# Retention's input projection in three passes on split operands, and the residual norms in two parts

## The chip, the cores and the metric

The kernel runs on one NeuronCore of a Trainium2 chip. The metric is the device time in microseconds (us) of one execution, as the median of several runs. The engines are TensorE (PE, with its weight loads as PEld), VectorE (DVE), ScalarE (ACT), GpSimd (POOL) and SyncE (SP), which issues most of the loads. Each runs its own instruction stream, and they meet only at semaphores.

## The reference, cut to what matters

Two blocks run one after the other on 512 tokens of width 1024. The first has two layers. A layer computes a mixer and then a feed-forward network, and each of the four is followed by a residual and a layer norm:

```python
for i in range(DEPTH):
    mod = (e @ ada_w[i] + ada_b[i])[:, None, :]
    sh1, sc1, g1, sh2, sc2, g2 = jnp.split(mod, 6, axis=-1)
    y = mixers[i % N_MIXERS](x * (1.0 + sc1) + sh1)
    x = layer_norm(DN_ALPHA * x + (1.0 + g1) * y, ln_g[i, 0], ln_b[i, 0])
    y = conv_ffn(x * (1.0 + sc2) + sh2, ffn_up[i], ffn_conv_w[i], ffn_conv_b[i], ffn_down[i])
```

(the second layer norm of a layer follows `conv_ffn` in the same way). The mixer of layer 1 is `retention`. Its input projection is `q, k, v, gate = jnp.split(h @ w_in, ...)`, with 1024 + 1024 + 2048 + 2048 columns: q and k are then turned by a rotary table, v is used by token, and gate goes through silu. The second block (a Hyena and HGRN2 mixer and a mixture of experts with 64 experts) is not touched by the change.

## The kernel before

Activations lie transposed in SBUF: `k.xT` holds the residual stream and `k.hT` the modulated input of the next matrix product, each as 8 tiles (KD) of 128 features by 512 tokens (T). Weights come in chunks through a ring of 4 slots (`NSLOT`): SP issues the load of chunk n as soon as chunk n-4 is used (`chunk_used`).

Most products of the first block use **split operands**. ACT rounds a chunk of weights to the matmul's reduced type (`round_chunk`, L373), POOL subtracts to get what is left and writes it back into the slot (`lower_chunks`, L378), and `SplitInput` does the same to the activations, tile by tile: ACT rounds (L455), DVE subtracts (L460). `products` then sums three passes for each input tile r: upper weights by upper input (L467), upper by lower (L468), lower by upper (L469). The projections of retention do without: `RetentionIn` multiplies plain 32-bit operands (L1460 by feature, L1471 by token), which TensorE runs as several passes inside. It takes 24 chunks of 256 columns: 8 for q and k (two groups of 128 features by 512 tokens each), 8 for v (by token: four groups of 128 tokens by 256 columns, so the weights move), 8 for gate (as q and k).

The order of stages is res0, up0, down0, rin (`RetentionIn`), heads, res1, up1, down1 and then the second block (`prepend` first). res0, down0, res1 and down1 are all `ResidualNorm`: 8 output tiles j of a product with 8, 22, 16 or 22 input tiles, each added to xT by DVE (L1237), and then the layer norm. In the norm PE sums the 8 tiles of xT to a mean (L1221), DVE subtracts it (L1245), ACT squares (L1268), PE sums the squares (L1225), ACT takes Ln and Exp (L1270, L1272), DVE scales (L1249), ACT applies gain and bias (L1275) and writes the modulated hT (L1285), and DVE multiplies xT by a constant (L1254). All stages end in `k.meet`, at which the four compute engines wait for one another. up0 and up1 are `FeedForwardUp`: 22 chunks, with convolution and gating on DVE (L1376, L1379, L1386), and in up0 a further table product on DVE (L680). Both start by splitting hT into their input.

## Time and profile before

| | |
|---|---|
| median of 3 runs | 4009.57 us (4006.97 to 4014.61) |
| the profiled execution's own time | 4000.63 us |
| its span in the profile | 3998.8 us |
| mean granted TensorE clock | 0.906 |

The profile is of one execution. Its rows give a start and a duration in us for an instruction (or for several alike, with xN), and in brackets how long the engine sat idle before it and whose signal ended that. A matmul's printed duration overlaps with its neighbours': what one costs in a row of many is the distance between starts. A plain 32-bit matmul appears as two records. res0 ends near 740, up0 runs to 1007, down0 with its norm to 1177, rin from 1184 to 1517, res1 with its norm to 1778, up1 to 2033, down1 with its norm to 2197, and the experts from about 2950 to the end.

### The profile page before, as it was taken

The page shows a single profiled execution, that of the slowest core. Times are in us where ns is not written, and L with a number is a line of the kernel's source. Part 1 is how long each engine was busy: PE and PEld are TensorE (multiplying, and loading weights), DVE is VectorE, ACT ScalarE, POOL GpSimd, SP SyncE. Part 2 cuts the span into 40 slices and gives each one's busy share as a digit, 9 for nine tenths or more (in the row PEclk, how much of TensorE's full clock was granted, in tenths as well). Part 3 has the DMA queues.
Part 4 walks back from the last instruction along what each step waited for, and adds up shares of the span by engine and source line. Part 5 has one row for each costly group of instructions (what it writes and reads, how often), then busy time and mean ns, then how long its engine had stood idle before and what let it go on. Part 6 is the DMA issues. An engine that isn't in the chain of part 4 may idle for free. (4 is left out here: it accounts for less than half of the span.)

```text
span 3998.8 us, 39863 instructions
## 1 busy us (share of the span) xinstructions
PE 3358.3 (84%) x15238; PEld 2171.1 (54%) x15238; DVE 1141.5 (29%) x1835; ACT 837.6 (21%) x1147; POOL 761.7 (19%) x363
## 2 busy tenths in 40 slices
PE   6988887799879998779988876899868888888886
PEld 3766775588744844558876775744343333333332
DVE  3524543566212002332231223544131111111112
ACT  2333223422220112332232333210100000000001
POOL 1422232233410001224442310200001111111110
PEclk8998888899989999889999875789979999999998
DMA  5233000355212212112230310110239999999996
GB/s 210 85 117 125 0 0 21 123 192 190 72 47 81 77 53 52 32 53 95 94 101 19 97 53 0 62 45 0 115 147 408 412 420 410 408 405 411 402 404 266
DMA packets 246141, 630.37 MB, mean 158 GB/s; under 512 B 18693, under 2 KB 192038, under 8 KB 221041
## 3 DMA queue, kind: packets, MB, share of 16 engines
q1 hardware_dynamic: 235249, 618.81, 41.1%
q0 software_dynamic: 10240, 8.43, 0.7%
q10 hardware_dynamic: 576, 2.10, 0.1%
q8 instruction: 49, 0.80, 0.1%
q14 instruction: 27, 0.22, 0.0%
HBM read 633.47 MB, written 20.97 MB: 164 GB/s over the span
## 5 line engine op out<-in xcount | busy, mean ns | idle before, releaser
L467 PE MATMUL ps<-arena_parts,arena_parts 128*128 128x512 f32 (+1 forms) x2016 | 750.6, 372 | 146.9 <-DVE hT_parts L460 65.5
L469 PE MATMUL ps<-arena_parts,ring_parts 128*128 128x512 f32 (+1 forms) x2016 | 743.7, 369 | 0.0
L378 POOL TENSOR_TENSOR ring_parts<-ring,arena_parts 128x2048 fp32r<-128x2048 f32 (+1 forms) x104 | 521.6, 5015 | 1085.7 <-ACT arena_parts L373 1085.7
L2773 PE MATMUL ps<-arena 128*64 128x512 f32 x1024 | 516.8, 664 | 161.4 <-DMA arena<-in_w_up 103.6
L468 PE MATMUL ps<-hT_parts,arena_parts 128*128 128x512 f32 (+1 forms) x1472 | 526.7, 358 | 0.0
L2774 PE MATMUL ps<-arena 128*64 128x512 f32 x1024 | 518.3, 665 | 0.0
L467 PEld LDWEIGHTS ps<-arena_parts,arena_parts 128*128 128x128 f32 x2016 | 383.5, 190 | 225.3 <-issue 112.9
L469 PEld LDWEIGHTS ps<-arena_parts,ring_parts 128*128 128x128 f32 x2016 | 383.4, 190 | 68.8
L2773 PEld LDWEIGHTS ps<-arena 128*64 128x64 f32 x1024 | 150.0, 152 | 496.0 <-issue 494.0
L468 PEld LDWEIGHTS ps<-hT_parts,arena_parts 128*128 128x128 f32 x1472 | 279.6, 190 | 41.1
L373 ACT ACTIVATE arena_parts<-ring 128x2048 fp32r<-128x2048 f32 (+1 forms) x104 | 208.8, 2008 | 382.4 <-PE ps L469 324.8
L2853 DVE TENSOR_SCALAR arena<-ps 128x256 f32<-128x256 f32 x64 | 27.2, 424 | 854.4 <-PE ps L2784 854.4
L1460 PE MATMUL ps<-hT,ring 128*128 128x512 f32 x512 | 222.4, 597 | 22.3 <-DMA ring<-in_ret_w_in 22.3
L2793 PE MATMUL ps<-arena 128*64 128x512 f32 x1024 | 233.8, 598 | 1.1 <-DVE arena L2853 0.6
L2693 POOL DMA_INDIRECT y_rows<-ring,y_of x64 | 64.7, 1011 | 855.4 <-ACT ring L2831 840.1
L468 PE MATMUL ps<-arena_parts,arena_parts 128*128 128x512 f32 x544 | 217.1, 399 | 0.0
L1460 PEld LDWEIGHTS ps<-hT,ring 128*128 128x128 f32 x512 | 98.0, 192 | 146.1 <-issue 146.0
L2837 ACT ACTIVATE arena<-ps 64x512 f32<-64x512 f32 x64 | 38.1, 595 | 649.0 <-PE ps L2774 649.0
L2774 PEld LDWEIGHTS ps<-arena 128*64 128x64 f32 x1024 | 149.9, 152 | 0.0
L2793 PEld LDWEIGHTS ps<-arena 128*64 128x64 f32 x1024 | 68.2, 136 | 114.8 <-issue 110.6
L2688 POOL DMA_INDIRECT ring<-x_rows,x_of x64 | 61.3, 958 | 334.5 <-DVEq L287 302.8
L1237 DVE SCALAR_TENSOR_TENSOR xT<-ps,mod,xT 128x512 f32 (+1 forms) x32 | 24.0, 751 | 332.1 <-PE ps L469 332.1
(446 smaller groups left out, 4028.0 us busy)
## 6 DMA issues: line engine op xcount, KB each, us to landing
arena<-in_w_gate SPq DMA_DIRECT2D x64, 2048.0 KB, 18.1
arena<-in_w_up SPq DMA_DIRECT2D x64, 2048.0 KB, 22.5
arena<-in_w_down SPq DMA_DIRECT2D x64, 2048.0 KB, 23.1
ring<-in_ffn_up SPq DMA_DIRECT2D x44, 1024.0 KB, 5.1
arena<-in_ada_w SPq DMA_DIRECT2D x20, 2048.0 KB, 9.9
ring<-in_ret_w_in SPq DMA_DIRECT2D x24, 1024.0 KB, 5.1
ring<-in_ffn_down SPq DMA_DIRECT2D x16, 1408.0 KB, 7.0
ring<-in_gdn_w_in SPq DMA_DIRECT2D x16, 1024.0 KB, 5.8
```

The costliest lines, as they stand in the source:

```text
L373: act.activation(self.upper(room, n, kt, cols), self.slot(n, kt, cols), ACT.Copy).then_inc(self.core.sem("chunk_rounded"), 1)
L378: pool.tensor_tensor(self.lower(n, kt, cols), self.slot(n, kt, cols), self.upper(room, n, kt, cols), ALU.subtract)\
L467: pe.matmul(out, upper[:, r], self.upper[r][:, part], start=(r == 0), stop=False)
L468: pe.matmul(out, upper[:, r], self.lower[r][:, part], start=False, stop=False)
L469: ins = pe.matmul(out, lower[:, r], self.upper[r][:, part], start=False, stop=(r == self.tiles - 1))
L1460: ins = pe.matmul(k.ps[:, g % 4, :], w[:, r, f * P:(f + 1) * P], k.hT[:, r, 0:T], start=(r == 0), stop=(r == KD - 1))
L2688: return pool.indirect_dma_start(m.xe[u], None, k.x_rows, at, bounds_check=T - 1, oob_is_err=False)
L2693: return pool.indirect_dma_start(k.y_rows, at, m.y_halves[u], None, bounds_check=2 * CHOICES - 1, oob_is_err=False)
L2773: pe.matmul(k.ps[upper, 2 + u, :], m.xeT[u][:, r, :], m.w_up[u][:, r, :], start=(r == 0), stop=(r == KD - 1))
L2774: ins = pe.matmul(k.ps[lower, 2 + u, :], m.xeT[u][:, r, :], m.w_gate[u][:, r, :], start=(r == 0), stop=(r == KD - 1))
L2793: ins = pe.matmul(k.ps[(upper, lower)[h], 6, :], m.actT[u][:, r, :], m.w_down[u][:, r, half], start=(r == 0), stop=(r == D_EXP // P - 1))
L2837: act.activation(m.silu[u], k.ps[SLOTS:2 * SLOTS, 2 + u, :], ACT.Silu).then_inc(self.sem("silu"), 1)
```

## The change

`RetentionIn` now uses split operands as well. ACT rounds and POOL subtracts each of its 24 chunks, and q, k and gate go through `products`. v is computed in four **pairs** of chunks: both chunks move together as 512 columns against 128 tokens of the input, again in three passes, into one bank for each group of 128 tokens. The first four chunks are loaded before the rope table and without waiting for the stage.

`ResidualNorm` is taken apart. While the product of the last output tile runs, PE sums the first seven tiles of xT with one matmul over a running total that DVE keeps (`origin`), and DVE and ACT centre and square those seven (centred on the mean of 7 tiles). The meet comes then, and a second part without a meet (`vector_tail`, `scalar_tail`, `tensor_tail`) adds and centres the last tile, corrects by the rest of the mean, takes the variance, and scales. ACT applies one combined gain and shift for each tile, twice (`upper` of the next stage's input, already rounded, and hT), and DVE subtracts to get `lower`. So up0, rin and up1 find their input split, and `prepend` no longer copies xT to hT. The first chunk of each following stage is rounded and split in the last chunk of the stage before (`following`; in `FeedForwardUp` the first chunk of the down projection).

```diff
+            if between and r == self.tiles // 2:
+                between()
             if first:
...
+        def origin():
+            self.wait(pe, "totalled", 1)
+            pe.matmul(k.ps[:, self.ORIGIN, :], k.ones[:], self.total, start=True, stop=True).then_inc(self.sem("mean"), 1)
...
-        self.wait(pe, "added", self.BANKS + KD)
-        for j in range(KD):
-            ins = pe.matmul(k.ps[:, 6, :], k.mean[:], k.xT[:, j, :], start=(j == 0), stop=(j == KD - 1))
-        ins.then_inc(self.sem("mean"), 1)
-        for j in range(KD):
-            self.wait(pe, "squared", j + 1)
-            pe.matmul(k.ps[:, 7, :], k.mean[:], self.square[:, j % 2], start=(j == 0), stop=(j == KD - 1)).then_inc(self.sem("var"), 1)
...
+        k = self.k
+        self.wait(pe, "centred", KD)
+        pe.matmul(k.ps[:, self.REST, :], k.mean[:], k.xT[:, KD - 1, :], start=True, stop=True).then_inc(self.sem("mean"), 1)
+        self.wait(pe, "totalled", 2)
+        pe.matmul(k.ps[:, self.VAR, :], k.mean[:], self.total, start=True, stop=True).then_inc(self.sem("var"), 1)
...
+    def centre(self, dve, j):
+        k = self.k
+        dve.scalar_tensor_tensor(k.xT[:, j, :], k.ps[:, self.ORIGIN, :], -1.0 / (D - P), k.xT[:, j, :], ALU.mult, ALU.add)\
...
+                self.add(dve, stream, n, c, f)
+                if j == 0:
+                    continue
+                a = k.xT[:, 0, :] if j == 1 else self.total
+                if j > 1:
+                    st.wait()
+                ins = dve.tensor_tensor(self.total, a, k.xT[:, j, :], ALU.add)
+                if j < KD - 2:
+                    st.done(ins)
+                else:
+                    ins.then_inc(self.sem("totalled"), 1)
...
+        stream.each(dve, self.chunks, self.per, tile, True)
         self.wait(dve, "mean", 1)
+        for step in range(KD + 1):
+            if step < KD - 1:
+                self.centre(dve, step)
+            if step >= 2:
+                self.add_square(dve, step - 1) if step < KD else None
...
+           .then_inc(self.sem("added"), 1)
         self.wait(dve, "added", self.BANKS + KD)
+        self.centre(dve, j)
+        self.add_square(dve, j)
+        self.wait(dve, "squared", KD + 1)
+        self.wait(dve, "summed", KD - 1)
+        dve.scalar_tensor_tensor(self.total, self.square[:, 0], -float(KD), self.total, ALU.mult, ALU.add).then_inc(self.sem("totalled"), 1)
         for j in range(KD):
-            dve.tensor_tensor(k.xT[:, j, :], k.xT[:, j, :], k.ps[:, 6, :], ALU.subtract).then_inc(self.sem("centred"), 1)
+            ins = dve.tensor_tensor(k.xT[:, j, :], k.xT[:, j, :], k.ps[:, self.REST, :], ALU.subtract)
+        st.done(ins)
+        st.wait()
         self.wait(dve, "rooted", 2)
+        for step in range(KD + 2):
...
+        if self.first:
+            self.input.scalar(act)
+        for c in range(self.first, self.chunks):
             stream.round_chunk(act, self.upper, stream.n + c, 0, self.kt, self.per * P)
             if c == 0:
                 self.input.scalar(act)
+        if self.following:
+            stream.round_chunk(act, self.upper, stream.n + self.chunks, 0, *self.following)
...
+    def scalar_tail(self, act):
+        k = self.k
+        self.take_square(act, KD - 1)
+        self.wait(act, "mean", 2)
+        self.wait(act, "summed", KD - 2)
+        act.activation(self.square[:, 0], k.ps[:, self.REST, :], ACT.Square).then_inc(self.sem("squared"), 1)
+        act.activation(self.one, k.eps[:, 0:1], ACT.Ln)
+        self.wait(act, "var", 1)
+        act.activation(self.inv, k.ps[:, self.VAR, :], ACT.Ln, bias=k.eps[:, 0:1]).then_inc(self.sem("rooted"), 1)
...
+            if self.next_input:
+                act.activation(self.next_input.upper[j], k.xT[:, j, :], ACT.Identity, bias=b, scale=a)
+            act.activation(k.hT[:, j, shown], k.xT[:, j, :], ACT.Identity, bias=b, scale=a).then_inc(self.sem("shifted"), 1)
...
-        self.input.vector(dve)
...
+                stream.round_chunk(act, self.upper, n + 1, i, FT, P)
...
+        def rope():
+            k.stage_over(sp, 9)
+            k.load_tables(sp, "rope", [(self.rope, k.tables["t_rope"])])
+
+        self.stream.load_run(sp, [tiles_of(k.ins["ret_w_in"])], KD, 2 * P, 3 * self.RUN, after_round=rope)
...
-                    for r in range(KD):
-                        ins = pe.matmul(k.ps[:, g % 4, :], w[:, r, f * P:(f + 1) * P], k.hT[:, r, 0:T],
-                                        start=(r == 0), stop=(r == KD - 1))
+                    at = slice(f * P, (f + 1) * P)
+                    ins = self.input.products(pe, k.ps[:, g % 4, :], upper[:, :, at], lower[:, :, at], first + g == 0)
...
+            stream.split_landed(pe, n + 1, 0, 2 * p + 1)
...
-                    ins = pe.matmul(k.ps[:, 4 + t, 0:2 * P], k.hT[:, r, t * P:(t + 1) * P], w[:, r, :],
-                                    start=(r == 0), stop=(r == KD - 1))
-                stream.group_done(ins, t == TT - 1)
-
-        stream.rounds(pe, self.RUN, 2, features("ret_rotated", 1))
-        stream.rounds(pe, self.RUN, TT, tokens)
+                    pe.matmul(out, self.input.upper[r][:, at], upper[:, :, r], start=(r == 0), stop=False)
+                    pe.matmul(out, self.input.upper[r][:, at], lower[:, :, r], start=False, stop=False)
+                    ins = pe.matmul(out, self.input.lower[r][:, at], upper[:, :, r], start=False, stop=(r == KD - 1))
...
-        stream.rounds(pe, self.RUN, 2, features("ret_gated", 2))
+        stream.each(pe, self.RUN, 2, features("ret_gated", 2, 2 * self.RUN), True)
...
+        for c in range(1, 3 * self.RUN):
+            pool.wait_ge(k.sem("chunk_rounded"), stream.splits + c + 1)
+            n = stream.n + c
+            pool.tensor_tensor(self.lower(stream, n, c), stream.slot(n, KD, 2 * P), self.upper(stream, n, c), ALU.subtract)\
+                .then_inc(k.sem("chunk_split"), 1)
...
-        k = self.k
-        for j in range(KD):
-            act.activation(k.hT[:, j, N_META:], k.xT[:, j, :], ACT.Copy)
+        pass
```

On ACT at the end of res0 (xT is the residual stream, hT the next input, ring a weight slot). Before:

```order
L1268 ACTIVATE arena<-xT 128x512 [waits residual_centred] x2
L1268 ACTIVATE arena<-xT 128x512 [waits residual_var,residual_centred] x6
L1270 ACT_TABLE_LOAD
L1270 ACTIVATE arena<-ps,eps 128x512 [waits residual_var]
L1272 ACT_TABLE_LOAD
L1272 ACTIVATE arena<-arena 128x512 [waits residual_rooted]
L1275 ACTIVATE xT<-xT,par 128x512 [waits residual_scaled] x2
L1285 ACTIVATE hT<-xT,mod 128x512 [waits residual_normed]
L1275 ACTIVATE xT<-xT,par 128x512 [waits residual_scaled]
```

and now:

```order
L376 ACTIVATE arena_parts_2048_2270<-ring 128x2048 [waits chunk_used,chunk_in_slot0]
L1358 ACTIVATE arena<-xT 128x512 [waits residual_centred] x2
L1358 ACTIVATE arena<-xT 128x512 [waits residual_summed,residual_centred] x5
L1358 ACTIVATE arena<-xT 128x512 [waits residual_summed,residual_centred,stage_ended]
L1378 ACTIVATE arena<-ps 128x512 [waits residual_summed,residual_mean]
L1379 ACT_TABLE_LOAD
L1379 ACTIVATE arena<-eps 128x1
L1381 ACTIVATE arena<-ps,eps 128x512 [waits residual_var]
L1383 ACT_TABLE_LOAD
L1383 ACTIVATE arena<-arena 128x512 [waits residual_rooted]
L1390 ACTIVATE arena_parts_512_81<-xT,arena 128x512 [waits residual_scaled]
L1391 ACTIVATE hT<-xT,arena 128x512
```

The rounding of up0's first chunk (L376) now stands ahead of the norm, seven of the eight squares stand ahead of the meet (`stage_ended`), and the split input (L1390) is written where xT's gain was applied.

On PE at the change from q and k to v in retention (a row of v before is one group of 128 tokens: 8 matmuls). Before:

```order
L1460 MATMUL ps<-hT,ring 128x512 x16
L419 REGISTER_ALU
L419 COMPARE_AND_BRANCH
L419 UNCONDITIONAL_BRANCH
L419 ISA
L1469 REGISTER_ALU
L1471 MATMUL ps<-ring,hT 128x256 x8
```

and now (the first of 32 input tiles of a pair's four groups, and the end of the one ahead):

```order
L496 MATMUL ps<-hT_parts_512_64,arena_parts_2048_2330 128x512
L497 MATMUL ps<-spare_parts_512_126,ring_parts_2048_1259 128x512
L435 REGISTER_ALU
L435 COMPARE_AND_BRANCH
L1613 MATMUL ps<-arena_parts_4096_117,ring_parts_512_119 128x512
L1614 MATMUL ps<-ring_parts_5632_3728,ring_parts_512_119 128x512
L1615 MATMUL ps<-arena_parts_4096_117,hT_parts_512_57 128x512
```

Each input tile takes three matmuls with 512 moving columns in place of one 32-bit matmul for each 256.

## Rows read from the trace of the kernel before

**Rows 1.** The page, busy totals and the granted clock in 40 slices.
```profile
PE 3358.3 (84%) x15238; PEld 2171.1 (54%) x15238; DVE 1141.5 (29%) x1835; ACT 837.6 (21%) x1147; POOL 761.7 (19%) x363
...
PEclk8998888899989999889999875789979999999998
```

**Rows 2.** Windows; columns: length, PE, PEld, DVE, ACT, POOL, granted clock, DMA, GB/s.
```profile
1184.00:1296.00 112.00, 112.00 (x258) 49.36 (x258) 26.43 (x42) 0.00 (x0) 0.00 (x0) 0.98 0.28 89
...
1296.00:1406.00 110.00, 110.00 (x511) 96.85 (x510) 3.77 (x6) 11.90 (x31) 0.00 (x0) 1.00 0.24 77
...
1406.00:1517.00 111.00, 110.29 (x258) 48.66 (x257) 0.00 (x0) 12.47 (x19) 0.00 (x0) 1.00 0.15 47
...
2960.00:3960.00 1000.00, 838.35 (x3814) 340.26 (x3813) 108.19 (x191) 75.67 (x127) 121.03 (x123) 0.93 0.98 400
```

**Rows 3.** Timeline from the first residual norm to the first feed-forward stage.
```profile
706.41 0.39 PE L469 MATMUL ps<-arena_parts,ring_parts 128*128 128x512 f32 x1
...
707.64 7.13 PE L1221 MATMUL ps<-xT,mean 128*128 128x512 f32 x16 [0.84 <-DVE xT L1237]
...
714.81 4.87 DVE L1245 TENSOR_TENSOR xT<-xT,ps 128x512 f32<-128x512 f32 x8 [7.23 <-PE ps L1221]
...
726.72 4.90 DVE L1249 TENSOR_TENSOR xT<-xT,arena 128x512 f32<-128x512 f32 x8 [7.03 <-ACT arena L1272]
...
728.87 0.80 ACT L1285 ACTIVATE hT<-xT,mod 128x512 f32<-128x512 f32 x1
...
741.82 13.16 DVE L460 TENSOR_TENSOR hT_parts<-hT,arena_parts 128x512 fp32r<-128x512 f32 x8 [2.53 <-ACT arena_parts L455]
...
746.54 0.77 PE L467 MATMUL ps<-arena_parts,arena_parts 128*128 128x512 f32 x1 [22.62 <-DVE hT_parts L460]
...
763.15 0.74 DVE L1376 TENSOR_SCALAR arena<-ps,par 128x512 f32<-128x512 f32 x1
```

**Rows 4.** Timeline of TensorE between the second norm and retention.
```profile
1143.62 0.40 PE L469 MATMUL ps<-arena_parts,ring_parts 128*128 128x512 f32 x1
...
1183.58 2.92 PE L1460 MATMUL ps<-hT,ring 128*128 128x512 f32 x3 [22.30 <-DMA ring<-in_ret_w_in]
```

**Rows 5.** Timeline of the first down projection's start, TensorE and GpSimd.
```profile
1017.58 0.77 PE L467 MATMUL ps<-arena_parts,arena_parts 128*128 128x512 f32 x1 [10.19 <-DVE arena_parts L460]
...
1024.64 11.54 POOL L378 TENSOR_TENSOR ring_parts<-ring,arena_parts 128x2816 fp32r<-128x2816 f32 x1 [7.76 <-ACT arena_parts L373]
...
1036.31 0.49 PE L467 MATMUL ps<-arena_parts,arena_parts 128*128 128x512 f32 x1 [1.69 <-POOL ring_parts L378]
...
1037.35 6.27 POOL L378 TENSOR_TENSOR ring_parts<-ring,arena_parts 128x2816 fp32r<-128x2816 f32 x1 [1.17 <-ACT arena_parts L373]
```

**Rows 6.** Timeline of the last norm's end, TensorE and ScalarE.
```profile
2169.45 0.40 PE L469 MATMUL ps<-arena_parts,ring_parts 128*128 128x512 f32 x1
...
2202.16 1.18 ACT L1658 ACTIVATE arena<-hT 128x528 f32<-128x528 f32 x2 [1.32 <-DVEq L287]
```

**Rows 7.** Timeline of the second feed-forward stage, DVE's group ends 48 passes apart.
```profile
1833.20 0.69 DVE L1386 TENSOR_TENSOR arena<-arena,ps 128x512 f32 x1 [4.87 <-PE ps L469]
...
1844.31 0.75 DVE L1376 TENSOR_SCALAR arena<-ps,par 128x512 f32<-128x512 f32 x1 [3.01 <-PE ps L469]
```

**Rows 8.** Timeline of TensorE at the half clock, two passes in a row.
```profile
1020.27 0.63 PE L467 MATMUL ps<-arena_parts,arena_parts 128*128 128x512 f32 x1
...
1020.70 0.44 PE L468 MATMUL ps<-arena_parts,arena_parts 128*128 128x512 f32 x1
```

**Rows 9.** Costliest groups and DMA issues, from the page.
```profile
L378 POOL TENSOR_TENSOR ring_parts<-ring,arena_parts 128x2048 fp32r<-128x2048 f32 (+1 forms) x104 | 521.6, 5015 | 1085.7 <-ACT arena_parts L373 1085.7
...
L373 ACT ACTIVATE arena_parts<-ring 128x2048 fp32r<-128x2048 f32 (+1 forms) x104 | 208.8, 2008 | 382.4 <-PE ps L469 324.8
...
L1237 DVE SCALAR_TENSOR_TENSOR xT<-ps,mod,xT 128x512 f32 (+1 forms) x32 | 24.0, 751 | 332.1 <-PE ps L469 332.1
...
ring<-in_ret_w_in SPq DMA_DIRECT2D x24, 1024.0 KB, 5.1
```

More of the change, by code:

```diff
@@ L298 @@
 ARENA_W = 30720
+W_PART = FT * P
+W_UPPER = ARENA_W - 2 * W_PART
 COLS = 32
@@ L379, in chunk @@
                 .then_inc(self.core.sem("chunk_split"), 1)
-        self.rounds(pool, chunks, per, chunk, True)
+        if first or following:
+            for c in range(first, chunks):
+                lower(self.n + c, 0, c, kt, cols)
+            if following:
+                lower(self.n + chunks, 0, chunks, *following)
+            self.skip(chunks, per, True)
+        else:
+            self.rounds(pool, chunks, per, lambda n, i, c: lower(n, i, c, kt, cols), True)
     def split_landed(self, pe, n, i, c):
@@ L399, in load_run @@
         rounds = chunks // NSLOT
+        if after_round:
+            for c in range(NSLOT):
+                one(c, 0, c)
+            after_round()
+            first = 1
         if rounds - first > 1:
@@ L434, in each, with skip_pairs @@
         self.skip(chunks, per, splits)
+    def skip_pairs(self, pairs, per):
+        self.n += 2 * pairs
+        self.groups += (per - 1) * pairs
+        self.splits += 2 * pairs
     def skip(self, chunks, per, splits=False):
@@ L654, in __init__ @@
         self.w = room.take(2, KD, self.W)
-        self.acc = acc_room.take(2, self.W)
+        self.acc = [acc_room.take(self.W) for _ in range(2)]
     def sync(self, sp, i, u):
@@ L1212, in chunk @@
                 j = c * self.per + f
-                self.wait(pe, "added", i * (NSLOT * self.per) + (j + 1))
+                self.wait(pe, "added", j + 1)
                 at = slice(f * P, (f + 1) * P)
-                ins = self.input.products(pe, k.ps[:, j % self.BANKS, :], upper[:, :, at], lower[:, :, at], c == 0 and f == 0)
+                ins = self.input.products(pe, k.ps[:, j % self.BANKS, :], upper[:, :, at], lower[:, :, at], j == 0, between=origin if j == KD - 1 else None)
                 stream.group_done(ins, f == self.per - 1)
-        stream.rounds(pe, self.chunks, self.per, chunk, True)
@@ new lines, in vector, with tile @@
+    def vector(self, dve, st, stream):
+        k, row = self.k, (2 * self.layer + self.norm) * KD
+        g, b = k.cols("ln_g", row, KD), k.cols("ln_b", row, KD)
+        self.input.vector(dve)
+        scale, shift, g_now, b_now = (self.affine[:, n] for n in range(4))
+        alpha = ALPHA if self.after else 1.0
+        dve.tensor_scalar(g_now, g, alpha, None, ALU.mult)
+        ins = dve.tensor_scalar(b_now, b, alpha, None, ALU.mult)
+        if self.after:
+            la, m = self.after
+            dve.tensor_tensor(scale, g, k.mod[:, la, m + 1], ALU.mult)
+            st.done(dve.tensor_tensor(shift, b, k.mod[:, la, m + 1], ALU.mult))
+            st.wait()
+            ins = dve.tensor_tensor(shift, shift, k.mod[:, la, m], ALU.add)
+        st.done(ins)
+        st.wait()
+        def tile(n, i, c):
@@ L1277, in scalar @@
[L1277 to L1286 removed]
+            a, b = self.affine[:, scale, j:j + 1], self.affine[:, shift, j:j + 1]
```

281 lines of the change are left out of this document (182 added, 99 removed).

## Prediction

> **What bounds the kernel now.** I read the page first. TensorE is busy for 84% of the span and no other engine for more than 29% [rows 1], but that is an average over stages, so I looked at windows. From 2960 us on, the experts' weights arrive at 400 GB/s with the DMA engines 98% busy [rows 2]. Nothing of that stage moves with the change: whatever the first block saves comes off the end. In the three runs of retention's projection TensorE is busy without a gap, for 112, 110 and 111 us at a granted clock of 0.98 to 1.00, while GpSimd does nothing at all [rows 2]. So there the price of the products is the time.
>
> The timeline between stages shows the other kind of time. After res0's last pass at 706.6 TensorE does only the norm's two sums, and then sits idle for 22.62 us until up0's first pass at 746.54 [rows 3]. The chain is serial: 16 records of mean sums (7.13), eight subtractions (4.87), squares and their sums, Ln and Exp, scaling, gain, modulation, the meet, and then the split of hT, in which eight DVE subtractions take 13.16 where eight of the same size take 4.90 a little earlier [rows 3]. up0's second group is evicted at 763.15 [rows 3]. Between down0 and retention the gap is from 1143.85 to 1183.58, ended by the load of the first weights, which waited for the stage [rows 4]. down0 starts after an idle 10.19 us, and waits once more for GpSimd before its second chunk [rows 5]. The last norm keeps the second block from 2169.7 to 2202.2 [rows 6].
>
> **The change, part by part.**
>
> *The price of a pass.* In up1, at full clock and with the same operands, two evictions that lie 48 passes apart are at 1833.20 and 1844.31 [rows 7], so a pass of 512 columns costs 11.11 / 48 = 0.2315 us. Retention has 16 chunks by feature with 2 x 8 x 3 passes (768) and 4 pairs by token with 4 x 8 x 3 (384), 1152 in all: 266.7 us. The trace does not show a token pass (the weights move in two pieces of 256). Its bounds are 0.2315, for the columns are as many, and 0.43, one 256-column plain product of now (110 us for 256 of them [rows 2]). I take 0.2315. The Trainium skill ("TensorE: Matmul & The Clock Gate", Back-to-back issue gap) gives the gap of isolated matmuls as N/2.4 + 2.5 ns, 0.216 for 512 columns. By it, the estimate for 1152 passes would be 18 us lower. The rows say 0.2315.
>
> *What feeds them.* Each chunk needs ACT for 2.0 us and then GpSimd for some 4.6 (6.27 for 2816 columns [rows 5], by width; 5.0 is the mean over all splits [rows 9]) in the 11.1 that TensorE takes for a chunk, and both engines were idle here or nearly so [rows 2]. A pair takes 22.2: its two loads come after the pair two ahead is used, at 5.1 us each [rows 9], so that the second split ends near 10.2 + 2.0 + 4.7 = 17. All 23 new splits are costed at nothing behind the products. What the cover is worth stands in the first rival.
>
> *The first group of retention* is fed by the norm: per tile ACT runs two activations, about 0.70 apart in a row (0.80 alone [rows 3]), 1.41 for a tile, against 0.69 for its three passes. Eight tiles take 7 x 1.41 + 0.7 = 10.6 instead of 5.6. I add 5.0 and a margin of 0.5 for chunk 1's split. Retention then runs 266.7 + 5.5 = 272 where it ran 333 (1183.6 to 1516.6 [rows 2, 4]): **61 gained**.
>
> *The norms.* Count from the last pass of the product. The sum over seven tiles is a plain matmul put into the last group: 0.9 (16 records in 7.13 [rows 3] are eight matmuls). It comes at half of the group's input tiles, so 2.8 us before the end with 8 tiles and 7.6 with 22. From its result DVE does 7 centrings and 6 additions of squares: 0.61 in a row (8 in 4.87 [rows 3]) and, for the form with a scalar, 0.75 alone [rows 9], 0.68 in a row, in sum 8.7. It ends 6.1 after a product with 8 tiles, 1.3 after one with 22 (in res1 with 16 tiles, 3.3). I take 6.1 for res0 and, keeping the difference as a margin, for res1 too. After the meet it is serial again: add and centre tile 7, 1.7; the rest of the mean on PE, 1.1; its square, 0.7 (the activation of the same size takes 0.80 [rows 3]); update of the total, 0.8; eight subtractions with the wait, 5.1, which cover the variance, Ln and Exp on PE and ACT (1.1 + 0.7 + 1.3 + 0.6); one scaling, 0.7; two activations, 1.6; one DVE subtraction, 0.7. That is 12.4, and 0.8 more at res0 and res1, where TensorE will have been idle for long enough to be at the half clock. First pass: 0.9 + 6.2 + 13.2 = 20.3 after res0's product, 0.9 + 1.4 + 12.5 = 14.8 after down0's.
>
> For res0 the second group of up0 then ends at 20.3 + 10.6 + 5.6 + 0.5 = 37.0, where it is 56.5 now (706.65 to 763.15 [rows 3]): 19.5, and for res1 the same: **39 gained**. For down0 the first pass comes after 14.8 where it is 39.7 [rows 4]: **25 gained**. For the last norm, scaling begins at 0.9 + 1.4 + 9.4 = 11.7, eight tiles follow ACT at 0.70, and the last multiplication, the copy of the prefix and the meet take 1.1 more: 19.1 where it is 32.5 [rows 6], since the copy to hT and the wait for small loads go: **13 gained**.
>
> *Down projections.* The first chunk's rounding and split now lie in the last chunk of up. TensorE's work before ends at 1007.4; with one tile rounded and subtracted (about 2 us) it starts at 1009.5 where it was 1017.58 [rows 5]. The second chunk becomes the limit. Its rounding ended at 1024.6 [rows 5] behind chunk 0's and 22 input tiles; without chunk 0's it ends near 1022. GpSimd then took 11.54 [rows 5], since DVE was still subtracting. DVE ends 8 us earlier now, so I take the length of the split after it, 6.3 [rows 5]: it starts at 1028.5 instead of 1036.31, 7.7 for each of down0 and down1: **15 gained**. Of the 8 us at the start only that much arrives.
>
> *At nothing:* the running total and the additions of squares inside the product (DVE sits idle for 3.0 to 4.9 us before an eviction [rows 7]); the combined gains (tiny); the rope table, which lands long before the first eviction; loops written out.
>
> Sum: 61 + 39 + 25 + 15 + 13 = 153. The profiled execution took 4000.6, so 3848; the median of the runs shown is 0.22% above it, which makes **3857**.
>
> **The rivals.**
>
> 1. *GpSimd and DVE get in each other's way.* The eight subtractions of 13.16 ran against two splits and lost 8.3 us, and the split of 11.54 lost 5.2 [rows 3, 5]. In retention the rotary work puts two-tensor operations beside each of the first eight splits, and after each norm eight multiplications of xT stand where chunk 1's split begins. If every split there took 11.54: 2.0 + 11.5 + 0.2 is 2.6 over TensorE's 11.1, seven times, 18; and 5.2 after three norms, 16. In sum 34: 3891. Against it: in up1 TensorE ran without a wait beside such work, group after group [rows 7]. The Trainium skill ("SBUF — State Buffer", Who interferes with whom) has an exclusive lock for the pair of ports that both use, when a DVE operation has two SBUF inputs; the 13.16 agrees. Chance 0.17.
> 2. *The norms' tails hide less.* If the sum over seven tiles came late, or the corrections waited for Ln and Exp, each of four norms would give back about 6: 3881. For it: the chain after the meet still has some ten handovers. Chance 0.12.
> 3. *The preparation does not hold.* If retention's loads still waited for the meet: 2.3 + 5.1 + 2.0 + 4.6 = 14.0, still before 14.8. This costs nothing, and has no chance of its own.
> 4. *The passes come closer together*, at 0.216: 18 less, 3839. Chance 0.03.
> 5. *Slower: the clock.* If TensorE ran at the half clock in retention, a pass would cost 0.43 (two starts at 1020.27 and 1020.70 [rows 8]), 0.198 more, in all 229: 4085. It decides at 153 / 0.198 = 773 of the 1152 passes. Against it: the granted clock is full in stages that keep TensorE as busy as this one [rows 2], and the slow stretches in the slices are where it idles [rows 1]. Chance 0.03.
>
> **How the numbers follow.** The forecast has 0.65 and its own range is 3845 to 3870 (margins of some 3 us in each of four norms and the unknown token pass). The range reaches into rivals 1 and 2: 3840 to 3884, which leaves out the clock, the closer passes and the worst of rival 1, less than 0.2. A measurement of this kernel can tell about 0.2% from no change. Faster by more: all cases but the clock, 0.96; within it 0.01; slower 0.03.
>
> **What the profile after would show.** Retention's projection near 272 us with passes 0.23 apart and no wait for GpSimd; 384 passes by token in 89 us; TensorE's first pass some 20 us after res0's product and 15 after down0's, then three passes each 1.4 us; the first pass of down0 2 us after up0, and a wait for GpSimd of 3 to 4 us before its second chunk. The prediction is wrong if splits in retention take over 9 us and TensorE waits for them, if token passes cost more than 0.24, or if DVE's chain around the meet is longer than 21 us for res0.

## The result, and the profile after

The changed kernel takes **3873.3 us** (3872.2 to 3874.7, 4 runs) where the kernel before, on the same chip, takes 4010.2 (4007.0 to 4014.6, 4 runs): ratio 0.9658, 95% interval 0.9641 to 0.9675. The forecast was 3857, its range 3840 to 3884. So 137 us came where 153 were expected. The profiled execution took 3872.23 us, its span is 3870.5.

From the page, busy totals and the new splits of retention. TensorE is busy for 86 us less than before [rows 1], GpSimd and VectorE for about 100 more each.

```profile
PE 3272.3 (85%) x15262; PEld 2179.7 (56%) x15262; DVE 1249.4 (32%) x1956; ACT 868.4 (22%) x1138; POOL 863.0 (22%) x387
...
L1701 POOL TENSOR_TENSOR ring_parts<-ring,arena_parts 128x2048 fp32r<-128x2048 f32 x23 | 107.0, 4660 | 174.4 <-ACT arena_parts L1668 174.4
```

Windows of retention's projection in thirds and of 1000 us in the experts (columns as in [rows 2]). TensorE is still busy nearly throughout (one wait of 1.23 us), but for 276 us and not 335; the experts' stage is what it was.

```profile
1148.00:1239.00 91.00, 87.97 (x365) 68.64 (x365) 69.88 (x62) 25.79 (x22) 42.40 (x9) 0.98 0.25 81
1239.00:1329.00 90.00, 90.00 (x392) 73.16 (x391) 7.67 (x6) 21.94 (x22) 32.33 (x7) 1.00 0.26 82
1329.00:1424.00 95.00, 92.70 (x399) 74.47 (x397) 0.00 (x0) 24.06 (x25) 33.36 (x9) 1.00 0.22 68
2827.00:3827.00 1000.00, 839.80 (x3806) 340.20 (x3808) 108.19 (x191) 75.08 (x126) 121.95 (x124) 0.92 0.98 400
```

TensorE's timeline, the row with which each stage begins, and its waits. The first is res0, 730.51 up0, 1006.79 down0, 1147.74 the retention, 1667.30 up1, 1922.50 down1, 2070.81 the first product behind the last norm.

```profile
660.24 0.77 PE L495 MATMUL ps<-arena_parts,arena_parts 128*128 128x512 f32 x1 [16.26 <-DVE arena_parts L486]
...
719.09 2.05 PE L1262 MATMUL ps<-xT,mean 128*128 128x512 f32 x2 [7.54 <-DVE xT L1275]
...
730.51 0.77 PE L495 MATMUL ps<-arena_parts,arena_parts 128*128 128x512 f32 x1 [5.89 <-DVE hT_parts L486]
...
738.88 0.50 PE L495 MATMUL ps<-arena_parts,arena_parts 128*128 128x512 f32 x1 [0.44 <-DVE hT_parts L486]
...
747.92 0.50 PE L495 MATMUL ps<-arena_parts,arena_parts 128*128 128x512 f32 x1 [1.11 <-POOL ring_parts L382]
...
766.33 0.79 PE L495 MATMUL ps<-arena_parts,arena_parts 128*128 128x512 f32 x1 [6.24 <-POOL ring_parts L382]
...
1006.79 0.76 PE L495 MATMUL ps<-arena_parts,arena_parts 128*128 128x512 f32 x1 [2.31 <-DVE arena_parts L486]
...
1025.68 0.51 PE L495 MATMUL ps<-arena_parts,arena_parts 128*128 128x512 f32 x1 [0.91 <-POOL ring_parts L382]
...
1147.74 0.77 PE L495 MATMUL ps<-ring_parts,arena_parts 128*128 128x512 f32 x1 [5.89 <-DVE hT_parts L486]
...
1667.30 0.77 PE L495 MATMUL ps<-arena_parts,arena_parts 128*128 128x512 f32 x1 [5.89 <-DVE hT_parts L486]
...
1922.50 0.48 PE L495 MATMUL ps<-arena_parts,arena_parts 128*128 128x512 f32 x1 [2.45 <-DVE arena_parts L486]
...
2070.81 9.57 PE L1846 MATMUL ps<-arena,mean 128*128 128x264 f32 x28 [11.42 <-ACT arena L1833]
```

Where 22.62 us of idle time stood before up0 [rows 3], there are waits of 7.54 and 5.89 with the sums of the norm between them. The stretches between these rows, beside the same ones of before (there res0 begins at 656.87, up1 at 1784.49, down1 at 2043.38, the product behind the last norm at 2202.94, the others are in [rows 3 to 5]; retention's heads begin at 1518.91 and 1424.22):

| from the first pass of ... to that of ... | before | after | change | forecast |
|---|---|---|---|---|
| start, res0 | 656.9 | 660.2 | +3.4 | 0 |
| res0, up0 | 89.7 | 70.3 | -19.4 | -19.5 |
| **up0, down0** | 271.0 | 276.3 | **+5.2** | **-8** |
| down0, retention | 166.0 | 141.0 | -25.0 | -25 |
| retention, its heads | 335.3 | 276.5 | -58.9 | -61 |
| heads, res1 | 133.7 | 134.2 | +0.5 | 0 |
| res1, up1 | 131.9 | 108.9 | -23.0 | -19.5 |
| up1, down1 | 258.9 | 255.2 | -3.7 | -8 |
| down1, product behind the last norm | 159.6 | 148.3 | -11.3 | -13 |
| from there to the end | 1795.9 | 1799.7 | +3.8 | 0 |

The rows add up to 128 us and not 137, because the profiled execution of the kernel before (4000.63) is 9.6 under the median of its runs. Against the forecast they are 25 short: 13 in up0, 4 in up1, 7 in the two ends that the change leaves alone and some 4 in four other rows, less 3.5 that res1 gave beyond it.

One row is off with its sign: up0 loses 5 where it should gain 8, and these are the 13. The other engines at up0's head show what is late (timeline; L1352 scales and shifts the residual stream, L708 is a product of the second conditioning, L1483 the eviction of a group, L1516 the Silu, L376 a rounding, L382 a split):

```profile
740.16 8.00 DVE L1352 TENSOR_SCALAR xT<-xT,arena 128x512 f32<-128x512 f32 x8
...
742.90 4.96 POOL L382 TENSOR_TENSOR ring_parts<-ring,arena_parts 128x2048 fp32r<-128x2048 f32 x1 [36.67 <-ACT arena_parts L376]
...
748.59 2.33 DVE L708 SCALAR_TENSOR_TENSOR arena<-arena,e 128x512 f32<-128x512 f32 x3
750.83 0.74 DVE L1483 TENSOR_SCALAR spare<-ps,par 128x512 f32<-128x512 f32 x1
...
759.10 0.72 ACT L1516 ACTIVATE arena<-spare,par 128x512 f32<-128x512 f32 x1 [3.50 <-DVE spare L1486]
759.73 1.89 ACT L376 ACTIVATE arena_parts<-ring 128x2048 fp32r<-128x2048 f32 x1
...
761.70 9.47 POOL L382 TENSOR_TENSOR ring_parts<-ring,arena_parts 128x2048 fp32r<-128x2048 f32 x2 [13.83 <-ACT arena_parts L376]
```

Read it from the end. TensorE waits at 766.33 for the split that begins at 761.70. GpSimd had been idle for 13.83 us; it waited for the rounding at 759.73. ScalarE could have rounded chunk 2 when chunk 0 was used, at about 747, but its queue had the Silu of chunk 0 ahead of it, and the second of them ran at 759.10. The Silu waited for VectorE, which evicted the first group, complete at about 741, only at 750.83. VectorE was still scaling the residual stream: eight instructions in 8.00 us, with a split on GpSimd from 742.90 to 747.86, and behind them it ran four operations of the second conditioning until 750.9. After the wait TensorE was at the half clock for a while: its passes start 0.43 apart from 766.92 to 769.48, and 0.83 was granted between 760 and 780. That wait and the slow passes make some 7.4 of the 13 us.

A second wait is new, at the other end of up0. The split of the down projection's first chunk, which the change has moved there, holds a product of the second conditioning (the first of the four in the third row takes 4.91 us), and TensorE waits 2.42 us for the last of them; the kernel before has no such wait in its last chunk.

```profile
994.18 6.28 POOL L382 TENSOR_TENSOR ring_parts<-ring,arena_parts 128x2816 fp32r<-128x2816 f32 x1 [12.11 <-ACT arena_parts L376]
...
995.49 0.69 DVE L1493 TENSOR_TENSOR arena<-arena,ps 128x512 f32<-128x512 f32 x1 [1.83 <-PE ps L497]
996.10 7.28 DVE L708 SCALAR_TENSOR_TENSOR arena<-arena,e 128x512 f32<-128x512 f32 x4
...
1003.43 1.05 PE L598 MATMUL ps<-ones,arena 128*128 128x1 f32 x8 [2.42 <-DVE arena L708]
```

### The profile page after: what moved, and what is told of

The parts are those of the page before. It is cut to its first block and busy times, and to the rows that moved or that the text cites. A ratio compares the mean times of both kernels' runs of the same rounds, so it can differ in the third digit from the quotient of the medians.

```text
span 3870.5 us, 39759 instructions
## 1 busy us (share of the span) xinstructions
PE 3272.3 (85%) x15262; PEld 2179.7 (56%) x15262; DVE 1249.4 (32%) x1956; ACT 868.4 (22%) x1138; POOL 863.0 (22%) x387
## 5 line engine op out<-in xcount | busy, mean ns | idle before, releaser
L495 PE MATMUL ps<-arena_parts,arena_parts 128*128 128x512 f32 (+1 forms) x2080 | 780.8, 375 | 109.0 <-DVE arena_parts L486 38.3
L497 PE MATMUL ps<-arena_parts,ring_parts 128*128 128x512 f32 (+1 forms) x2080 | 771.1, 371 | 0.0
L382 POOL TENSOR_TENSOR ring_parts<-ring,arena_parts 128x2048 fp32r<-128x2048 f32 (+1 forms) x105 | 516.0, 4915 | 1057.4 <-ACT arena_parts L376 1057.4
L496 PE MATMUL ps<-hT_parts,arena_parts 128*128 128x512 f32 (+1 forms) x1728 | 630.1, 365 | 0.0
L495 PEld LDWEIGHTS ps<-arena_parts,arena_parts 128*128 128x128 f32 x2080 | 396.5, 191 | 200.0 <-POOL ring_parts L382 56.7
L497 PEld LDWEIGHTS ps<-arena_parts,ring_parts 128*128 128x128 f32 x2080 | 396.9, 191 | 71.5
L496 PEld LDWEIGHTS ps<-hT_parts,arena_parts 128*128 128x128 f32 x1728 | 329.3, 191 | 51.7
L376 ACT ACTIVATE arena_parts<-ring 128x2048 fp32r<-128x2048 f32 (+1 forms) x105 | 210.6, 2007 | 377.7 <-PE ps L497 340.8
L1701 POOL TENSOR_TENSOR ring_parts<-ring,arena_parts 128x2048 fp32r<-128x2048 f32 x23 | 107.0, 4660 | 174.4 <-ACT arena_parts L1668 174.4
L496 PEld LDWEIGHTS ps<-arena_parts,arena_parts 128*128 128x128 f32 x544 | 104.3, 192 | 26.2 <-issue 1.0
L708 DVE SCALAR_TENSOR_TENSOR arena<-arena,e 128x512 f32<-128x512 f32 x84 | 114.0, 1358 | 2.6
```

The lines of the kernel that those rows point to most:

```text
L376: act.activation(self.upper(room, n, kt, cols), self.slot(n, kt, cols), ACT.Copy).then_inc(self.core.sem("chunk_rounded"), 1)
L382: pool.tensor_tensor(self.lower(n, kt, cols), self.slot(n, kt, cols), self.upper(room, n, kt, cols), ALU.subtract)\
L495: pe.matmul(out, upper[:, r], self.upper[r][:, part], start=(r == 0), stop=False)
L496: pe.matmul(out, upper[:, r], self.lower[r][:, part], start=False, stop=False)
L497: ins = pe.matmul(out, lower[:, r], self.upper[r][:, part], start=False, stop=(r == self.tiles - 1))
L708: ins = dve.scalar_tensor_tensor(self.acc[u], self.w[:, u, r, :], v, self.acc[u], ALU.mult, ALU.add)
```

## The experiments

Twelve runs followed, two of the changed kernel and ten of nine variants, each timed beside the kernel before (4006.6, 4007.5 and 4005.8 us in the three sets). "Touched stretch" is from res0's first pass to the product behind the last norm: 1410.6 us in the changed kernel, 1546.1 before. One part of it that no variant touches, from the heads to res1, is 131.9 to 134.2 us long in these profiles, so a difference of 2 us in the whole stretch says nothing.

### The changed kernel again, two times

> The changed kernel as it stands, run again beside its variants, so that a difference of a few us is read on one chip. Expected by every theory: 3873 us within 4, and between the first pass of up0 and the first of down0 again 276 us, where 263 were forecast (271.0 before less 8). If that stretch came out at 265 or less here, the 13 us missing there would be an accident of one execution and nothing of the kernel.

> The changed kernel once more, as the mark for the three runs beside it: 3873 us within 4. The stretch from the first pass of res0 to the first product behind down1's norm (that is, all that the change touches) was 1410.6 and 1411.1 us in the two executions seen, and is expected within 2 of that, while the start of the kernel ahead of it was 656 to 665 in nine executions and is expected anywhere in that.

Measured: 3873.3 us (3865.6 to 3877.0, 4 runs) and 3876.0 (3866.0 to 3876.6, 5 runs). Touched stretch 1411.1 and 1410.6, up0's 276.3 both times. So the 13 us belong to the kernel, and so does the wait at up0's end (2.44 both times). Beside the kernel before, the gains are 133 and 130 us. In the first of them the wait took another form, VectorE's timeline:

```profile
744.60 3.74 DVE L1352 TENSOR_SCALAR xT<-xT,arena 128x512 f32<-128x512 f32 x8
...
748.77 4.94 DVE L708 SCALAR_TENSOR_TENSOR arena<-arena,e 128x512 f32<-128x512 f32 x1
...
755.20 0.74 DVE L1483 TENSOR_SCALAR spare<-ps,par 128x512 f32<-128x512 f32 x1
```

The eight take 3.74 here, and one product of the second conditioning behind them takes 4.94 where its like take 0.75; its group is evicted 20.25 us after up0's first pass, in the first profile 20.32. In these two profiles it costs the same, whichever instruction GpSimd's split holds.

### Each half of the change alone

```diff
 # the kernel before, with
-        class RetentionIn: whole operands, hT as it is
+        class RetentionIn of the change; it splits its input itself
```

> The kernel before, with the retention's input projection of the changed one and nothing else: three passes on split operands, pairs of chunks of the values; the norms and the feed-forward stay as they were. The input is split at the head of the stage, since no norm prepares it. The forecast's term for the passes is 61 us from the first pass of the projection to the first of the heads (1152 passes at 0.2315 us and 5 for the first group); here the passes start later, by the rounding of the first chunk and its split (about 10 us, as at the starts of the other stages before), which the kernel before didn't have: 3952 to 3962, a gain of 48 to 58. If the gain in the changed kernel came only with the prepared input, this one would gain less than 40.

Measured: **3949.9** (3946.8 to 3959.1), a gain of 57.7. The first pass comes after 22.69 us of idle time, 166.4 after down0's first as before (166.0), so the rounding and split of the first chunk cost next to nothing beside the old norm; the heads follow 278.3 later.

```profile
1192.14 0.76 PE L495 MATMUL ps<-ring_parts,arena_parts 128*128 128x512 f32 x1 [22.69 <-DVE hT_parts L486]
```

```diff
 # the changed kernel, with RetentionIn of before
+                        if g == 0 and per_chunk == 1:
+                            self.norm.wait(pe, "shifted", r + 1)
                         ins = pe.matmul(..., k.hT[:, r, 0:T], ...)
```

> The changed kernel with the retention's input projection of before: four-cycle products on whole operands, nothing of it prepared by the norm; the norms taken apart, the starts of up and down by the previous stage stay. By the forecast's terms (two norms of 19.5, the middle one 25 where the first pass now waits for the norm's tiles, the last 13, less the 13 us that went missing in up0): 72 to 82 us gained, so 3928 to 3940. The two halves alone should add up to the whole (137): if they give more than 145 together they share a cost, if less than 125 they need one another.

Measured: **3931.1** (3927.3 to 3934.4), a gain of 76.4; the projection takes 335.3 as before. 57.7 and 76.4 make 134.1, against gains of 137, 133 and 130 us of the whole in its three sets; in the touched stretch they make 56.9 + 75.0 = 131.9 against 135.5. The halves add up within some 4 us.

### Chunks of the values by one and by two

```diff
-        for p in range(self.PAIRS):      # 4 x 4 x 24 passes, 512 columns
+        for c in range(self.RUN):        # 8 x 4 x 24 passes, 256 columns
```

> The changed kernel with the values' products by single chunks: 768 passes that move 256 columns where the change has 384 that move 512, everything else as it is. If a pass costs what its columns cost (0.2315 us for 512, so 0.116 for 256), there is no difference: 3873 within 3, and the pairs are worth nothing. If each pass of 256 is held by the load of its weights (some 0.19 us each as the weight loads of the changed kernel show), 768 take 146 us instead of 89: 3925 to 3935. Between them a fixed cost for each pass would show.

Measured: **3876.3** (3873.6 to 3880.8), the projection 278.1 us against 276.5. TensorE's timeline in that stretch:

```profile
1300.02 0.28 PE L1613 MATMUL ps<-arena_parts,arena_parts 128*128 128x256 f32 x1
1300.14 0.28 PE L1614 MATMUL ps<-ring_parts,arena_parts 128*128 128x256 f32 x1
...
1301.91 0.28 PE L1614 MATMUL ps<-ring_parts,ring_parts 128*128 128x256 f32 x1
```

16 passes in 1.89 us, 0.118 each, half of a pass of 512. The pairs are worth 1.6 us in this stretch; it is the three passes that pay.

### The preparation of the down projections

```diff
-            else:
-                stream.round_chunk(act, self.upper, n + 1, i, FT, P)
```

(and the same split on GpSimd; `first=0` in down0 and down1)

> The changed kernel without the preparation of the down projections in the up stage: the first chunk of ffn_down is rounded and split at the head of its own stage, twice. The forecast gave each start 7.7 us; what was seen is 2.3 to 2.5 us before the first pass instead of some 10. If the term is right, this is 13 to 17 us slower than the changed kernel (3886 to 3890). If the preparation only moved a wait (the second chunk is waited for all the same, and the split at the end of up stands in the way of its last group), 3873 to 3880.

Measured: **3882.4** (3882.0 to 3888.8), 6 to 9 slower than the changed kernel in the other sets (it was not timed in this one). down0 begins after 10.25 us idle where it was 2.31. up0's stretch is 5.3 longer and up1's 7.8; with down0 (0.7 longer) and down1 (1.1 shorter) that is 12.7. The touched stretch as a whole is only 10 longer (1420.9), because the part from the heads to res1, which this edit does not touch, is 2.3 shorter here. Both expectations come true in part. The preparation pays, but the rival is there too: without it TensorE's wait of 2.42 us at the end of up0 is gone, and that is the difference between 5.3 in up0 and 7.8 in up1, which has no conditioning product.

### What is late in up0

```diff
             stream.round_chunk(act, self.upper, n + 1, i, KD, 2 * P)
-            if c % 2:
+            if c % 2 == 0:
                 return          # else the two Silu of the even chunk
```

> Two chunks of ffn_up make a pair; ScalarE rounds the next chunk and then runs the two Silu of an even chunk, so the rounding of chunk 2 stands in its queue behind the Silu of chunk 0. Here the Silu are issued one step later, behind the rounding of chunk 2. Theory A (the queue): the 13 us missing in up0 come from that order, since the Silu of chunk 0 wait for VectorE, which evicts late because it still scales the residual stream. Then the 6.24 us wait for GpSimd's split at 766 us and the half clock behind it go, and the whole is 9 to 13 us faster than the changed kernel (about 3862), up0's stretch 264 to 268 us, up1's 1 to 3 shorter. Theory B (VectorE and GpSimd hold each other up on their shared access, whatever the order): nothing moves in the order of splits, 3870 to 3875. Theory C (the half clock at 773 to 781 comes by itself, the wait being small): the wait goes, 5 to 6 us gained, up0's stretch 270.

Measured: **3867.0** (3860.1 to 3868.2), 6.2 less than the changed kernel in its set; touched stretch 1402.6, up0's 269.4. ScalarE and GpSimd:

```profile
746.26 1.91 ACT L376 ACTIVATE arena_parts<-ring 128x2048 fp32r<-128x2048 f32 x1 [4.14 <-PE ps L497]
757.13 1.28 ACT L1516 ACT_TABLE_LOAD   x1 [8.95 <-DVE spare L1486]
...
748.25 4.88 POOL L382 TENSOR_TENSOR ring_parts<-ring,arena_parts 128x2048 fp32r<-128x2048 f32 x1 [0.16 <-ACT arena_parts L376]
```

Chunk 2 is rounded when chunk 0 has been used, and split at once; the wait of 6.24 is gone, and so are the passes at the half clock there. The gain is the number of theory C, but not its mechanism, since the slow passes went with the wait. Theory B falls, for the order alone moved the split. Theory A asked for more than there was: VectorE is as late as before (the Silu follow at 757), TensorE waits 1.92 us for chunk 1's split, which takes 5.83 us beside VectorE's work (4.60 where the scaling is gone, below), and passes 0.43 apart turn up near the end of the stage (982.9 to 986.3). The order also does something that no theory had: down0's first chunk is rounded and split earlier (983.33, 16 us before the stage's end, where it was 12.6), and the wait of 2.42 at the end of up0 is gone as well.

```diff
-        for j in range(KD):      # end of the norm's tail
-            dve.tensor_scalar(k.xT[:, j, :], k.xT[:, j, :], self.affine[:, 2, j:j + 1], ...)
+    def scale_stream(self, dve):      # called in down0, RetentionIn, down1
+            dve.tensor_scalar(k.xT[:, j, :], k.xT[:, j, :], self.kept[:, 0, j:j + 1], ...)
+        self.kept = self.sb("kept", [P, 2, 2, KD])
```

> The eight instructions that scale and shift the residual stream are taken out of the norm's tail and issued a stage later, behind the input's split in down0 and down1 and behind the rotations in the retention; all of it is still computed. Theory A (the queue): they take 8.0 us of VectorE at the head of up0 against 3.7 where GpSimd is idle, and everything that hangs on the first eviction comes 8 us later for it. Without them group 0 is evicted near 743 and not 751, the Silu of chunk 0 end 8 us sooner, and the wait of 6.24 us at 766 shrinks to nothing: 7 to 12 us faster than the changed kernel (3861 to 3866). Theory B (the two engines hold each other up): the split of chunk 1 (4.96 us) gets 1 to 2 us shorter, and the gain is no more than that, 3871. Theory D (the eviction's delay is harmless, since PE has four banks): no change within 1.5 us, and at the start of down0 up to 4 us lost where the eight now stand.

Measured: **3853.6** (3850.0 to 3861.2), 19.6 less; touched stretch 1399.2, up0's 268.3, up1's 252.5. VectorE and GpSimd at up0's head, and where the eight now stand in down0:

```profile
738.14 4.60 POOL L383 TENSOR_TENSOR ring_parts<-ring,arena_parts 128x2048 fp32r<-128x2048 f32 x1 [36.62 <-ACT arena_parts L377]
...
738.19 0.75 DVE L1494 TENSOR_SCALAR spare<-ps,par 128x512 f32<-128x512 f32 x1
...
1006.40 6.94 DVE L1363 TENSOR_SCALAR xT<-xT,kept 128x512 f32<-128x512 f32 x2
...
1006.60 6.46 POOL L383 TENSOR_TENSOR ring_parts<-ring,arena_parts 128x2816 fp32r<-128x2816 f32 x1 [18.93 <-ACT arena_parts L377]
```

The first eviction comes 12.45 us after the first pass and not 20.3. In down0 two of the eight take 6.94, as long as the split beside them, and the eight with two splits some 15.6; down0's stretch is still 140.8, since no eviction is due. Theory A holds in the stretch (11.4 less, 7 to 12 expected), B and D fall; the other 8 us of the time no theory had. The wait at the end of up0 is still there (2.44).

> The later scaling and the Silu behind the rounding together; everything is computed. Theory A: both cure the same wait, so that the gains don't add: 9 to 14 us faster than the changed kernel (3859 to 3864), up0's stretch 262 to 267 us. If they did add (18 us or more, below 3856), there would be two separate waits, and theory A, which knows one, would be short of a second cause. Theory B: as the changed kernel, 3870 to 3875.

> The later scaling and the Silu behind the rounding, again, beside the changed kernel itself: 18 to 22 us faster than it by the medians if the first result holds, with 1397 us within 2 in the touched stretch (14 less than the changed kernel). If start and end only scattered in its favour, the difference is 12 to 16.

Measured: **3852.3** (3849.8 to 3859.2) and **3852.4** (3850.3 to 3858.8), 5 runs each, ratio to the kernel before 0.961 (0.960 to 0.963) both times. Touched stretch 1397.2 and 1397.1, up0's 266.6, up1's 252.4. The cures don't add in full: 6.9 and 8.0 in up0 make 9.7 together. Both remove the wait at up0's head, as theory A has it; but the order alone removes the one at its end, so there are two waits, and theory A knew one. By its time (below 3856) this run also met the condition set for two waits, though 8 us of that lie outside the stretch. This is the fastest version, 21 and 24 us under the changed kernel in its sets.

But the touched stretch is shorter by 13.5 only. Two more kernels asked where the rest comes from.

```diff
+        self.kept = self.sb("kept", [P, 2, 2, KD])      # never used
```

> The changed kernel with the small tile of kept constants (128 bytes in each partition) allocated and never used; its instructions are the changed kernel's. The later scaling was 19.6 us faster by its times but only 12 in the stretch that it touches. Theory E: the tile moves every tensor allocated behind it, and that alone is worth the other 8 us: about 3865 here. Theory F: the other 8 are the scatter of the kernel's start and end, which differ by up to 9 and 8 us between executions: 3873 within 4.

Measured: **3863.0** (3861.6 to 3871.8), 13 less than the changed kernel beside it and 10 less than in the set before; four of its five runs are below all nine repeats of that kernel (3865.6 at least). Its touched stretch is 1409.8, so whatever it gains lies outside. Its profiled execution was its slowest and shows no place for it. That is theory E's number, though not explained.

```diff
+        if self.after:
+            return      # the eight scalings left out
```

> The changed kernel without the eight scalings of the residual stream after res0, down0 and res1, and without the tile of constants; that part of the computation is left out, the last norm keeps its own. By the queue theory their place at the head of the stage is what costs, not their work: as the later scaling in the touched stretch (1399 us within 3) and, by theory F, in its time the changed kernel's less 12 to 16 (3857 to 3861). By theory E 8 more than the later scaling has, 3861 to 3865. If the work of the eight does cost something where they stand later, this one is 3 or more below the later scaling.

Measured: **3859.2** (3855.3 to 3865.8), touched stretch 1401.7, up0's 268.9. Without the tile, it gains 14 to 17 by its time and 9 in the stretch: theory F's number. Taken alone the two runs point different ways. All runs together lean to theory E: the median time less the touched stretch is 2453.2 to 2455.2 us in the four runs that have the tile, and 2460.1 to 2465.5 in the nine that don't and compute everything, the kernel before among them. The kernel without the scalings lies between, at 2457.5. As the later scaling is not slower than this, the work of the eight costs nothing where it stands there.

## Why the prediction was right, and where it fell short

**Retention's passes: right.** 1152 passes at 0.2315 us and 5.5 for the first group made 272; it took 276.5 up to the heads' first product, which stands 2.3 behind the point to which the 333 of before were counted, so 274. No split is waited for: the 23 take 4.66 us in the mean, not the 9 at which the prediction would have failed. The open term, the token pass, came out at its lower bound (384 passes in 88.4 us, 0.231 each, where 89 was said), and by single chunks it would have too.

**Norms: right.** First pass 20.3 us after res0's product was forecast; it was 19.1 (711.38, which is the last start and a pass of 0.23, to 730.51), and the stretch to it shrank by 19.4. res1 gave 23.0: the margin of 3 us that I kept there was not needed. down0's norm gave 25.0 of 25, the last 11.3 of 13. The first group of each stage is fed at 1.41 us a tile, as worked out (737.48, 738.88), and up0's second group ends 35.3 after res0's product where 37.0 was forecast.

**Down projections: right in kind, too large.** The first pass comes 2.3 us behind the last sums, as said (2), and the wait for the second chunk is 0.9 in down0 and 1.7 in down1 (3.1 there in a repeat), less than the 3 to 4 forecast. Undone, both together cost 6 to 9 by the times and 12.7 in the stages concerned, where 15 were booked. What the sum left out is that the moved split holds VectorE's conditioning product at the end of up0: 2.42 us of waiting.

**What failed: all work behind up0's second group was put at nothing.** I priced the tail up to the second group of up0, and there it was right: chunk 1's passes begin at 747.92, 17.4 after the first, wait included. I costed nothing behind that point. Rival 1 named the very place (eight operations on xT where chunk 1's split begins) and a price of 5.2, and put it on the split; that split took 4.96, and the price fell on VectorE instead (8.00 for 3.74), and did not stop there. A late eviction delays two Silu, these stand in ScalarE's queue ahead of the rounding of chunk 2, and that one feeds GpSimd and TensorE. The two cures show both halves: with the order of the queue changed, up0 is 6.9 shorter, with VectorE free, 8.0, with both, 9.7. Part of the first and the last figure is the wait at up0's end, which the order removes too. Of the 13 missing, 3.6 stay. In the first run with both cures a wait of 1.38 us for the conditioning's sums at 976.84 is followed by passes 0.43 apart for 3.4 us, which costs some 1.5 us (the kernel before has that wait too, 1.34 at 994.33, without slow passes behind it); 0.7 is a wait for chunk 1's split; the rest I have not placed. In up1, 4 us are missing, and 2.8 of them come back with both cures.

**The rivals.** 1 happened in part and through a queue: most of the 13 us of up0 and some of the 4 of up1, not 34. In retention it did hold VectorE, and TensorE waited for that once, 1.23 us, since two splits in a row held two operations of the rotation:

```profile
1222.59 4.60 DVE L1640 TENSOR_TENSOR arena<-arena 128x512 f32 x1
1227.12 5.08 DVE L1641 TENSOR_TENSOR arena<-arena 128x512 f32 x1
...
1232.31 0.50 PE L495 MATMUL ps<-ring_parts,arena_parts 128*128 128x512 f32 x1 [1.23 <-DVEq L1643]
```

2 did not happen, 4 and 5 neither. The forecast's case had 3845 to 3870 for itself; the result lies 3 above, in the part of the range that came from rival 1.

**The clock of the sum.** I put the median 0.22% over the profiled execution. The changed kernel's profiled time and median agree within 1.1 us in the first set. The parts that the change leaves alone were 7 us longer in this profile; over thirteen executions of it and its variants the start was 656.0 to 664.7 and the end 1792.8 to 1804.5, so 7 is scatter. Some 5 of the end's 12 us are one spell at the half clock: in seven of the fourteen profiles it is granted for 13.7 us from some 511 us behind the last norm (2581.9 to 2595.6 us in the second repeat of the changed kernel), in the other seven it is not granted there.

**Open.** With an unused tile of 128 bytes in each partition the median was 10 to 13 us lower, outside the touched stretch, and all four runs with the tile agree. It moves the tensors allocated behind it; whether a transfer or an engine gains by that, and which, was not found. Of the 21 us of the fastest version, 13 are shown by the trace, and some 8 go with the tile.

## What to carry to other kernels

When a chain is shortened, ask what stands in the queues at its new end: work that used to run in idle time (here the scaling of the residual stream) now meets the next stage's first eviction. An engine's queue passes delays on to work that has nothing to do with them, so put what feeds the bound engine (a rounding) ahead of what only follows it (a Silu), when its input is ready first. And look at the stretch as a whole after the change, not only at the gap that was closed: 19 us were won before up0 and 13 of what was to follow were lost inside it.

## What the runs showed of the hardware

- In the rows of VectorE read here, a split on GpSimd under way holds an operation whose operands all lie in SBUF until the split is over: eight `tensor_scalar` on 512 columns take 3.74 us alone and 8.00 with 4.96 of a split in them; a `scalar_tensor_tensor` takes 0.75 and 4.94; two `tensor_scalar` beside a split of 6.46 take 6.94. One that takes an operand from PSUM is not held: in the changed kernel's profile, nine evictions (L1483) that begin inside a split take their usual 0.75, and L1493 at 995.49 its 0.69. They are late only when they stand behind a held one. It goes the other way too: the split of 11.54 us in [rows 5] begins in a row of VectorE's subtractions, and these keep their 0.68 while it takes 5.3 longer than the next. The Trainium skill ("SBUF — State Buffer", Who interferes with whom) has the shared pair of ports as an exclusive lock, taken by `tensor_scalar` too in its two-port mode; the rows of held operations agree.
- The profile's 188 ns for a weight load does not space passes: 256-column passes start 0.118 us apart with a load each.
- Passes of 512 columns on split operands start 0.2308 (by token) to 0.2327 us (by feature) apart in retention, whether the columns come from one buffer or two.
- TensorE's granted clock fell behind some short waits and not behind others of the same length: behind 6.24 us, passes 0.43 apart for 2.6 us; behind 1.97 us at 753.22 in the first repeat of the changed kernel, for 3.4; behind 1.92 us at 748.15 with the Silu later, none.
